# A two-layer transformer step on one core: the first blocks with products of ones ahead, the wide matmuls first, and one square sum

## The reference

```python
def rmsnorm(x, g):
    xf = x.astype(jnp.float32)
    y = xf * lax.rsqrt(jnp.mean(xf * xf, axis=-1, keepdims=True) + EPS)
    return (y * g.astype(jnp.float32)).astype(x.dtype)
...
    a = rmsnorm(h, attn_norm[i])
    proj = a @ w_in[i]
    aq, af, ai, ag, bq, bk, bv, bf, cq, ck, cv = jnp.split(proj, split_idx, axis=-1)
```

## Time and profile before

| | |
|---|---|
| Median of 3 runs | 2250.62 us (2249.77 to 2250.86) |
| The profiled execution | 2249.81 us, its span 2248.0 us |
| TensorE busy | 2229.4 us, 99% of the span |
| VectorE busy | 1846.6 us, 82% |
| ScalarE busy | 1167.1 us, 52% |
| DMA | 228 GB/s over the span |

### The profile page before, as it was taken

How to read it: one execution, slowest core, us unless ns; L and a number is a source line. 1 busy time by engine, 2 the same in 40 slices (tenths; PEclk the granted TensorE clock), 3 DMA queues, 4 the chain that set the end, 5 groups by cost and what they waited for, 6 DMA issues and landing times.

```text
span 2248.0 us, 34334 instructions
## 1 busy us (share of the span) xinstructions
PE 2229.4 (99%) x12802; PEld 1967.3 (88%) x12802; DVE 1846.6 (82%) x2873; ACT 1167.1 (52%) x1709; POOL 111.3 (5%) x211
## 2 busy tenths in 40 slices
PE   8999999999999999999999999999999999999998
PEld 7888889888888888888899899989988888888887
DVE  7887989889889898988889888998766666666666
ACT  6554665555445454454457568656644444434344
POOL 0000000000111111111010000000000000000000
PEclk9999999999999999999999999999999999999999
DMA  8556654568888888888875554556655555555553
GB/s 318 187 181 248 235 218 159 184 243 302 307 294 309 293 304 314 293 302 299 302 273 180 201 211 151 188 191 227 238 182 194 187 187 197 187 197 188 190 200 116
DMA packets 86883, 515.61 MB, mean 229 GB/s; under 512 B 9781, under 2 KB 10341, under 8 KB 37584
## 3 DMA queue, kind: packets, MB, share of 16 engines
q1 hardware_dynamic: 57168, 405.82, 49.7%
q0 software_dynamic: 28992, 106.43, 13.8%
q10 hardware_dynamic: 576, 1.31, 0.2%
HBM read 511.39 MB, written 2.14 MB: 228 GB/s over the span
## 4 chain that ended last, share of the span: by engine, by line
PE 96%; DVE 3%; ACT 1%; issue 0%; DMA 0%; SPq 0%; ACTq 0%; DVEq 0%
PE ps L584 24%; PE ps L598 12%; PE ps L658 10%; PE ps L906 8%; PE ps L908 8%; PE ps L907 8%; PE ps L663 5%; PE ps L655 3%; PE ps L654 3%; PE ps L656 3%; PE ps L692 1%; PE ps L690 1%; PE ps L691 1%; PE ps L735 1%; PE ps L745 1%; DVE wl L1667 1%
## 5 line engine op out<-in xcount | busy, mean ns | idle before, releaser
L1667 DVE TENSOR_TENSOR wl<-raw,wh 128x1024 fp32r<-128x1024 f32 x762 | 928.9, 1221 | 303.5 <-ACT wh L1105 301.1
L1105 ACT ACTIVATE wh<-raw 128x1024 fp32r<-128x1024 f32 x766 | 805.7, 1056 | 637.2 <-PE ps L908 310.2
L584 PE MATMUL ps<-xs,wh 128*128 128x512 f32 x1744 | 418.0, 391 | 0.0
L584 PEld LDWEIGHTS ps<-xs,wh 128*128 128x128 f32 x1744 | 320.5, 188 | 62.0
L1775 DVE CUSTOM_DVE_ANT_0 modraw<-modraw,cb 128x1024 f32<-128x1024 f32 x192 | 233.0, 1218 | 11.3 <-DMA modraw<-in_wmod 10.9
L598 PEld LDWEIGHTS ps<-xs,wl 128*128 128x128 f32 x1744 | 224.1, 191 | 8.8
L598 PE MATMUL ps<-xs,wl 128*128 128x256 f32 x1744 | 226.9, 283 | 0.0
L658 PE MATMUL ps<-xs,wh 128*128 128x512 f32 x880 | 223.5, 396 | 0.0
L658 PEld LDWEIGHTS ps<-xs,wh 128*128 128x128 f32 x880 | 158.3, 189 | 29.8 <-issue 0.6
L584 PE MATMUL ps<-xc,wh 128*128 128x512 f32 x608 | 150.2, 389 | 0.0
L534 POOL DMA_DIRECT2D modraw<-in_wmod x172 | 90.8, 528 | 1040.3 <-DVE modp L1775 1037.1
(11 more groups left out here) (368 smaller groups left out, 3548.5 us busy)
## 6 DMA issues: line engine op xcount, KB each, us to landing
raw<-in_w SPq DMA_DIRECT2D x381, 1024.0 KB, 5.1
modraw<-in_wmod POOLq DMA_DIRECT2D x192, 512.0 KB, 4.8
x<-in_x SPq DMA_DIRECT2D x4, 512.0 KB, 9.1
raw<-in_w SPq DMA_DIRECT2D x4, 512.0 KB, 8.9
tbias<-rel_rows POOLq DMA_DIRECT2D x4, 512.0 KB, 6.8
cb<-c_silu POOLq DMA_DIRECT2D x1, 1024.0 KB, 5.0
g2row<-g_rows POOLq DMA_DIRECT2D x1, 1024.0 KB, 10.5
finrow<-in_fin POOLq DMA_DIRECT2D x1, 1024.0 KB, 4.9
```

The lines of the kernel that those rows point to most:

```text
L584: m = nc.tensor.matmul(PS[(b + bi) % 4][:, :], hi[:, t * P:(t + 1) * P], src[k].rearrange("p a t -> p (a t)"), start=opens and first and n ...
L1105: nc.scalar.activation(wh[:, h % HS, :], raw[:, u % RAW, (h % 2) * 1024:(h % 2 + 1) * 1024], ACT.Copy).then_inc(s_round, 1)
L1667: nc.vector.tensor_tensor(wl[:, h % HS, :], raw[:, (h // 2) % RAW, (h % 2) * 1024:(h % 2 + 1) * 1024], wh[:, h % HS, :].bitcast(F32), ALU. ...
```

## The change

TensorE gets 15 products of ones by ones (128x128, float32) ahead of its first run, as soon as the parameters are loaded; their result in bank 7 is read by nobody. Each of the runs 1 to 7 now has all its wide matmuls first and then all its low ones, as run 0 had in two portions; the low half is waited for only behind the wide ones, and runs 4 to 7 end with the wide matmul of the last tile. The squares of x are merged: VectorE adds each group to the one before (`other`) and makes 256 columns once, after the fourth group. TensorE sums them once, in run 7 behind the wide ones. So the square of group 2 or 3 waits for the merge of the group before it (`s_sqr`) and no longer for the 256 columns of the group two before.

```diff
-        FIRST_BLOCKS, ENTRY_SUMS = 4, {5: (0, 1), 6: (2,), 7: (3,)}
+        LEAD_IN = 15
+        FIRST_BLOCKS, ENTRY_SUM = 4, 7
...
-        SUMS = lambda n: n + 3 if n else 0
-        summed_to = lambda n, i=0: sqs[:, n % 2, :] if n else sqs[:, i, :]
-        MERGES = lambda n: 3 * (n - 1) if n else 0
+        SUMS = lambda n: n
+        summed_to = lambda n: sqs[:, n % 2, :]
+        MERGES = lambda n: 3 * n
...
+                    def high(k, stop=False):
+                        return nc.tensor.matmul(PS[t][:, :], hi[:, k * P:(k + 1) * P],
+                                                XPAIR[8 * q + k].rearrange("p a t -> p (a t)"),
+                                                start=q == 0 and k == 0, stop=stop)
+
+                    def low(k):
+                        return nc.tensor.matmul(PS[t][:, 0:T], lo[:, k * P:(k + 1) * P], XPAIR[8 * q + k][:, 0, :],
+                                                start=False, stop=False)
+
                     pe.wait_ge(s_round, h + 1)
-                    if h:
-                        pe.wait_ge(s_split, h + 1)
...
+                    for first, end in ((0, 4), (4, 8)) if h == 0 else ((0, 8),):
+                        for k in range(first, end - 1 if q and end == 8 else end):
                             if t == 0:
                                 pe.wait_ge(s_xs, XS["attn"] + 8 * q + k + 1)
...
+                            high(k)
+                        if h == ENTRY_SUM:
+                            square_sums(N_ATTN)
+                        pe.wait_ge(s_split, h + 1)
+                        if q and t == 0:
+                            pe.wait_ge(s_xs, XS["attn"] + 16)
+                        for k in range(first, end):
+                            m = low(k)
+                    if q:
+                        m = high(7, stop=True)
                     m.then_inc(s_used, 1)
...
             pe.wait_ge(s_ones, 1)
+            pe.wait_ge(s_par, 16)
+            for _ in range(LEAD_IN):
+                nc.tensor.matmul(PS[7][:, 0:P], ones[:, :], ones[:, :], start=True, stop=True)
             first_blocks()
...
-                if n == 0 and g >= 2:
-                    act.wait_ge(s_sqs, g - 1)
-                elif g >= 2:
+                if g >= 2:
                     act.wait_ge(s_sqr, MERGES(n) + g - 1)
...
-                if n and g:
+                if g:
                     nc.vector.tensor_tensor(pair, pair, other, ALU.add).then_inc(s_sqr, 1)
                     dve.wait_ge(s_sqr, MERGES(n) + g)
-                if not n or g == 3:
-                    if n:
-                        dve.wait_ge(s_ssq, max(4, SUMS(n - 1)))
-                    nc.vector.tensor_tensor(summed_to(n, g), pair[:, 0, :], pair[:, 1, :], ALU.add).then_inc(s_sqs, 1)
+                if g == 3:
+                    if n >= 2:
+                        dve.wait_ge(s_ssq, SUMS(n - 1))
+                    nc.vector.tensor_tensor(summed_to(n), pair[:, 0, :], pair[:, 1, :], ALU.add).then_inc(s_sqs, 1)
```

More of the change, by code:

```diff
@@ L696, in token_unit, with square_sums @@
                     c.n["b"] += TOK_BANKS[width]
-            def square_sums(n, i=0):
-                pe.wait_ge(s_sqs, SUMS(n) + i + 1)
-                nc.tensor.matmul(PS[4][:, 0:T], ones[:, :], summed_to(n, i), start=i == 0, stop=i == (0 if n else 3)).then_inc(s_ssq, 1)
+            def square_sums(n):
+                pe.wait_ge(s_sqs, SUMS(n) + 1)
+                nc.tensor.matmul(PS[4][:, 0:T], ones[:, :], summed_to(n), start=True, stop=True).then_inc(s_ssq, 1)
             def head_norm(m, i):
@@ L802, in first_blocks @@
                     q, t = divmod(h, FIRST_BLOCKS)
-                    for g in ENTRY_SUMS.get(h, ()):
-                        square_sums(N_ATTN, g)
                     hi, lo = wh[:, h % HS, :], wl[:, h % HS, :]
-                    pe.wait_ge(s_round, h + 1)
-                    if h:
-                        pe.wait_ge(s_split, h + 1)
[L809 to L812, removed]
+                    def high(k, stop=False):
+                        return nc.tensor.matmul(PS[t][:, :], hi[:, k * P:(k + 1) * P],
+                                                XPAIR[8 * q + k].rearrange("p a t -> p (a t)"),
+                                                start=q == 0 and k == 0, stop=stop)
@@ L813, in first_blocks @@
+                    def low(k):
+                        return nc.tensor.matmul(PS[t][:, 0:T], lo[:, k * P:(k + 1) * P], XPAIR[8 * q + k][:, 0, :],
+                                                start=False, stop=False)
+                    pe.wait_ge(s_round, h + 1)
+                    for first, end in ((0, 4), (4, 8)) if h == 0 else ((0, 8),):
+                        for k in range(first, end - 1 if q and end == 8 else end):
                             if t == 0:
                                 pe.wait_ge(s_xs, XS["attn"] + 8 * q + k + 1)
-                            last = q == 1 and k == 7
```

## The result

The changed kernel takes **2255.25 us** in the median of 13 runs (2254.11 to 2257.31), the one before 2250.45 us on the same chip (13 runs, 2249.58 to 2250.92). The ratio is 1.0022, with a 95% interval of 1.0014 to 1.0029: 4.8 us slower. I had said 2254.6. The profiled execution took 2254.7 us, its span 2252.9.

What follows compares the result with a forecast made beforehand. TensorE was taken to bound the kernel, so run 8's start decides: 4.0 us later through the loop, TensorE's savings worth nothing, giving 2253.8 us, or 2254.6 on the median; range 2252.6 to 2257.2.

Steps and rivals of the forecast that it cites:

- run 0: TensorE's first run of the first blocks (runs 0 to 7), 4.28 us before; the lead-in was to save 0.6 us there.
- The loop: ScalarE and VectorE take turns (square, round, low half, halve, merge); run 8 starts at 39.70 instead of 35.66, 4.0 us later.
- The three waits: TensorE waits 1.7 us for run 7's rounding, 1.3 for the square sum, 2.4 for block 0's bank.
- What TensorE saves is worth nothing: Savings of 0.6 (lead-in), 1.3 (one square sum) and 0.1 us (wide first) lie in front of the new waits.
- Does it come back, or grow?: Behind run 8: VectorE catches up at 73.33, low half 20 keeps 0.5 us, the 4.0 us neither returns nor grows.
- The sum: Whole execution: 2249.81 us plus 4.0 is 2253.8; on the median 2254.6 us, 0.18% more.
- rival 1: TensorE's clock falls in the new idle times, costing up to 1.45 us: 2256.1 us; chance 18%.
- rival 4: Something behind run 8 runs out of lead (low half 20, ScalarE's table loads): up to 1 us more, 2255.6; chance 6%.
- a quarter of the forecast's chance: Part of the forecast's 64% counted, with rivals 1 and 4, toward slower by over 0.2% (over 2255.1 us), 0.39.
- against 2: Rival: the loop binds only once, run 8 starts 1.6 us late at 37.3: 2252.2 us; chance 7%.
- (3): Rival: no wait for the merges, TensorE's gain at run 8 stands: 2249.8 to 2250.4 us; chance 5%.

Runs made afterwards that it cites:

- r5: Kernel before with one number changed: squares of groups 2 and 3 wait for the sum of the group just before; 2253.79 us, 1.0014.
- r3: Changed kernel with two more square buffers, so the squares of groups 2 and 3 wait for no merge; 2250.45 us, 1.0002.
- r2: Changed kernel without the lead-in of 15 products of ones; 2255.51 us, 1.0021 against the kernel before.
- r7: Changed kernel's lead-in and matmul order, but no merges: four sums in runs 6 and 7 and the old waits; 2249.35 us, 0.9996.
- r6: Kernel before with only the lead-in of 15 products of ones added; 2249.67 us, 0.9995.
- r8: r3 with VectorE's three operations for the silu of c moved from step 5 to step 7; 2250.08 us, 0.9997.
- r9: r3 with the silu of c moved to step 19, where VectorE is idle; 2248.62 us, 0.9994.
- r1: The changed kernel measured again, no edit; 2255.71 us, 1.0022 against the kernel before.
- r4: Changed kernel with 5, 3 and 7 products of ones filling idle times ahead of run 7, square sum and run 8; 2254.55 us, 1.0019.

## Why the prediction was right, and where it was not

**The loop: right in kind, and in size to 0.7 us.** I had square 2 at 25.77, square 3 at 30.57, the sum at 35.15, run 8 at 39.70. The trace has 26.22, 31.11, 35.81 and 40.40. Of these 0.70 us at run 8, 0.34 are a later landing of x (15.48 against 15.14), which shifts all that stands behind it; from that landing to run 8 it is 24.92 us, 4.40 more than before and not 4.04. The other 0.36 are mostly handovers: my sum set 0.03 from each of three roundings to its low half, and it is 0.10 (round 6 is done at 28.43, 27.39 plus 1.04, and the low half starts at 28.53); it set 0.09 from the taken bank to run 8, and it is 0.16. r5 shows the wait as the cause, and r3 its removal as the cure.

**The three waits: right.** 1.64, 1.23 and 2.23 us for 1.7, 1.3 and 2.4, each at the place and with the releaser named. I did not list the small one of 0.47 us at run 6, though my own times imply it.

**What TensorE saves is worth nothing: right.** r2 shows it for the lead-in, r3 for everything together: 1.96 us in one idle time. The lead-in ended at 9.54, inside my bounds of 6.8 to 10.1. Its pieces are 0.21 us apart up to 8.56 and 0.11 from 8.71 on; my 0.224 for the slow ones was an estimate, twice the 0.112 of the earlier trace rows. Run 0 took 3.64 us (10.24 to 13.88) instead of 4.28, the 0.6 that I had. Worth nothing it is only with the merges: without them (r7) run 8 comes 0.8 us earlier. r6 shows that the lead-in alone does not give that; between the order of matmuls and the place of the sums no run decides.

**"Does it come back, or grow?": the step that failed.** I took the slack of VectorE for the slack of the kernel: at 73.33 VectorE waits 1.96 us for ScalarE, so it "has caught up". It has not. In the changed profile the same row stands 5.05 us later with the same idle time, since ScalarE's rounding stands in its program behind two of its operations that wait for VectorE. VectorE's timeline and ScalarE's there:

```profile
78.38 2.36 DVE L1666 TENSOR_TENSOR wl<-raw,wh 128x1024 fp32r<-128x1024 f32 x2 [1.96 <-ACT wh L1106]
```

```profile
75.33 1.06 ACT L1288 ACTIVATE sec<-sec 128x1024 f32<-128x1024 f32 x1 [1.24 <-DVE kq L2031]
76.29 1.04 ACT L1289 ACTIVATE kq<-kq 128x1024 f32<-128x1024 f32 x1
77.24 1.99 ACT L1106 ACTIVATE wh<-raw 128x1024 fp32r<-128x1024 f32 x2
```

So VectorE's whole delay of 5.05 us reaches the second meeting with TensorE. In the trace of the kernel before, VectorE's and TensorE's timelines have it so:

```profile
90.39 1.22 DVE L2060 TENSOR_TENSOR sec<-sec,kq 128x1024 f32<-128x1024 f32 x1
```

```profile
91.66 2.05 PE L764 MATMUL ps<-sec,kk 128*128 128x128 f32 x16
```

The operand is done at 91.61 and TensorE takes it at 91.66: no slack at all, a place that I had not looked at, because a list of waits doesn't show what comes just in time. In the changed kernel the two rows are:

```profile
95.44 1.21 DVE L2059 TENSOR_TENSOR sec<-sec,kq 128x1024 f32<-128x1024 f32 x1
```

```profile
96.71 2.05 PE L765 MATMUL ps<-sec,kk 128*128 128x128 f32 x16 [0.34 <-DVE sec L2059]
```

TensorE, 4.74 us late, waits 0.34 more. The step is worth 0.3 us here, and more in r8, where this meeting took 1.0 us back and low half 20 the other 0.4.

**The sum.** 4.74 at run 8 and 0.3 at 92 us make 5.05; the spans differ by 4.9 (2252.9 less 2248.0), where I had 4.0. Counted from x's landing it is 4.71 us at the second meeting (96.71 less 15.48, against 91.66 less 15.14), and behind it both kernels take 2156 us to within 0.2. The medians say less: 2254.45 us for the executions without a fall of the clock is 4.0 over 2250.45. The profiled execution of before lies 0.6 under its median, that of the changed kernel 0.25 over these 2254.45, partly because x's landing moves single executions (14.80 to 15.48 over all profiles); the rest of this difference is not explained. So it is in part luck that the forecast of 2254.6 lies only 0.65 us under the measured median. A slip in adding: rivals 1 and 4 and a quarter of the forecast's chance are 0.40, not 0.39.

**The clock: mis-sized in its chance.** I gave rival 1, at 2256.1 us, 18%, because 2.4 is nearer to 0.5 than to 9.9. By the mean clocks it came in 13 of 24 executions. Its price, 1.45 us, was near: 1.56 in one profile (3.65 less 2.09) and 1.3 by the medians. The measured median of 2255.25 lies between the forecast and the rival, because it is taken over both sorts. The other rivals did not come: the loop bound twice (against 2), no gain stood (3). Of rival 4's kind was the second meeting, at another place than the one named; the one named, low half 20, ran out of its lead only in r8.

## What to carry to other kernels

A buffer that is released one step later looks harmless, but if the releaser stands in a program behind something that needs the waiter's next step, two engines take turns (here the roundings stood 4.91 and 4.69 us apart where they had stood 2.67 and 1.99); follow such a wait round until it comes back to its own engine. An idle time of an engine is slack only if what ends it doesn't itself depend on that engine: look at what the releaser waited for. And a gain at one meeting of two engines lasts, as r8 and r9 show, only if the engine that sets the time of the next meeting has gained as much.

## What the runs showed of the hardware

- TensorE's granted clock read 0.53 over 40.40:44.00 behind three idle times of 1.64, 1.23 and 2.23 us in the profile of r1, with the wide matmuls there 0.42 to 0.50 us apart, and 1.00 behind the same three in another execution of the same program, with 0.22 to 0.30 us between them; by the mean clocks it fell in 13 of 24 executions. With idle times of 0.59, 1.23 and 2.23 us (r2) it was 6 of 11, with one of 1.96 us ahead of run 8 (r3) 3 of 11, with 1.09, 0.89 and 1.17 us (r5) none of 11, with 0.67 at most from run 0 on (r4) none of 11. Behind the same idle times it fell in some executions and not in others.
- The pace does not rise at the same time in every execution: the lead-in's 15 products, started at 3.46 to 3.55 us in all nine profiles that have them, took between 5.00 us (r7, the pieces 0.21 us apart up to 6.38 and 0.11 from 6.52 on) and 6.53 us (r1, 0.21 apart up to 9.65).
- The record of the granted clock is not complete: the window of the earlier trace rows reads 1.00, though the wide matmuls of that stretch start 0.43 to 0.56 us apart (9.90, 10.46, 10.89), against 0.23 behind 13.02 and in run 8, while the fall in r1 reads 0.53.
- The landing of x's third group lies between 14.80 and 15.48 us in the profiles, and what stands behind it moves with it. From landing to run 8 the changed kernel has 24.92 and 24.93 us in two executions and r2 24.92, the kernel before and r6 20.52 and 20.52: measured from there, 0.1 us can be told apart.
